# Half of the last matrix product by Strassen's seven block products, with its weight sums made in the opening

## The chip, the cores and the metric

The kernel runs on one core of a Trainium2 chip. Its engines are named as in the profile: PE (TensorE, matrix products), ACT (ScalarE), DVE (VectorE), POOL (GpSimd) and SP (SyncE, which here issues nearly all DMAs). Each runs its own list of instructions in order, and they meet through semaphores. The metric is the device time of one execution in microseconds (us), lower is better.

## The reference, cut to what matters

```python
h = _rmsnorm(x, g_pre)                       # x is 1024 x 1024, float32
proj = h @ w_in
...                                          # stick-breaking attention, gated linear attention
y_sb, y_gla = ... @ w_o_sb, ... @ w_o_gla
g_sb, g_gla = sigmoid(gate_logits + b_gate)  # two 1024 x 1024 gates
merged = g_sb * y_sb + g_gla * y_gla
x = x + merged @ w_out                       # the last product, 1024 x 1024 by 1024 x 1024
return _rmsnorm(x, g_final)
```

All is float32. The kernel gets there by splitting every operand into a high part (the PE's rounded fp32r form) and a low part (what is left of it), and by three passes: high by high, high by low, low by high. A product of a 128x128 block by a 128x512 block is so three matmuls.

## The kernel before, in words

The program has one hand-written instruction list for each engine. The stages are:

1. The opening (to about 59 us): x is loaded and normalised by rows (`row_norms` on ACT, `norm_rows` on DVE), turned by PE, and split into `h_hi` and `h_lo` (`h_high`, `h_low`). PE makes the first three column tiles of the projection (`first_tile`). POOL makes some constants.
2. The attention pairs, the gated linear attention, and the two products with `w_o`, whose outcome goes to a scratch in DRAM.
3. Seven of the eight tiles of the two gates (`gate_block(v, j)`, v from 0 to 6, j from 0 to 6). These already go by seven block products in place of eight. After each tile DVE merges: `mT` holds `merged` transposed, 8 blocks of 128 rows by 1024 columns, one block for each gate tile. Block 0 is the last to be finished. In the last gate tile SP also loads `w_out` in 8 chunks (`load_wout`), ACT makes the high parts (`wout_high`) and DVE the low parts (`wout_low`).
4. The last product: for each of 8 row tiles t and 2 column halves e, PE sums 8 blocks k in three passes, 24 matmuls of 128x512 into one bank of a ring of four (line 942). Before tile t, ACT splits columns 128 t to 128 t + 128 of `mT` into `m_hi` (line 1326) and DVE into `m_lo` (line 1837), two buffers in turn. The very first tile takes the blocks in the order 7 to 0, so that block 0 comes last; its piece of 128 columns is split apart (`split_m0(1)`, lines 1213 and 1741) as soon as DVE has merged block 0 (`merge_last`, lines 1844 and 1846). After each tile DVE adds x (`row_sum`, line 1861), ACT squares and sums the row and takes the root, DVE scales by it and by `g_final` (line 1875), SP stores.

What sets the order around the last product: PE waits for `mt_lo` (the low part of `mT`), for `wout_l` (the low part of `w_out`), and for `o5_free` (a bank read out). POOL has one instruction in this stage: it spreads `g_final` over the partitions (`partition_broadcast`, line 577), for which DVE waits (`fin_bc`).

POOL's operations do not all lie in the code that it holds at one time. The instruction order shows a row `ISA` with no operands where other code is called for: once ahead of the first `affine_select` (line 559) and once ahead of `partition_broadcast` (line 577). In the trace these are two records MODIFY_POOL_CONFIG each.

Of the kernel before, what the change touches and what calls it, by code (L numbers as in the profile page):

```python
# [12 lines left out]
P = 128  # L13
# [5 lines left out]
D = 1024  # L19
# [109 lines left out]
Y_LAST = 37  # L129
Y_SB_BANKS = 18  # L130
# [23 lines left out]
def stickbreak_gla_hybrid(nc, x, g_pre, w_in, b_gate, w_alpha_up, b_alpha_up, g_gla_norm,  # L154
# [8 lines left out]
    with ExitStack() as ctx:  # L163
# [98 lines left out]
        x_res = at("x_res", F + 20, [P, 2, D])  # L262
        y_row = at("y_row", F + 32, [P, 2, D])
        y_out = at("y_out", 8, [P, 2, D])
        g_fin = at("g_fin", F + 72, [P, D])
        junk5 = at("junk5", F + 76, [P, D])
        g_fin_row = at("g_fin_row", 4, [1, D])

        y_dram = nc.dram_tensor("y_scratch", (NP, 2, P, SEQ), F32, kind="Internal").ap()

# [101 lines left out]
        wout_l = sem("wout_l")  # L372
        fin_loaded = sem("fin_loaded")
# [38 lines left out]
        def _(sp):  # L412
# [19 lines left out]
            for c in range(8):  # L432
                sp.dma_start(w_up[RANK * c:RANK * (c + 1), :], w_alpha_up[0]).then_inc(up_loaded, 16)
# [75 lines left out]
            def load_wout(c):  # L509

                e, kk = c // 4, 2 * (c % 4)
# [16 lines left out]
            def store(t):  # L528
                for e in range(2):
                    es = slice(HALF * e, HALF * e + HALF)  # L530
                    sp.wait_ge(y_done, 2 * t + e + 1)
                    sp.dma_start(out_rows[t][:, es], y_out[:, t % 2, es]).then_inc(stored[t % 2], 16)
# [4 lines left out]
            for t in range(ST):  # L537
                if t >= 2:
                    sp.wait_ge(o5_free, 2 * (t - 2) + 2)
                else:  # L540
                    sp.wait_ge(prod_done, NP * NP)
                sp.dma_start(x_res[:, t % 2, :], x_rows[t]).then_inc(xr_loaded[t % 2], 16)
                if t >= 1:
                    store(t - 1)
            sp.wait_ge(tail_out, 1)
            sp.dma_start(out_rows[ST - 1][:, 0:HALF], y_out[:, 1, 0:HALF]).then_inc(stored[1], 16)
            sp.wait_ge(y_done, 2 * ST - 1)
            sp.dma_start(out_rows[ST - 1][:, HALF:D], y_out[:, 1, HALF:D]).then_inc(stored[1], 16)
            for s in stored:
                sp.wait_ge(s, 16 * ST)  # L550
# [807 lines left out]
        def _(dve):  # L1358
# [86 lines left out]
            for part in range(2):  # L1445
                stack(0, part, part)
# [468 lines left out]
```

## Time and profile before

| | us |
|---|---|
| median of 3 runs | 822.37 (822.10 to 822.48) |
| the profiled execution's own time | 822.67 |
| its span, first to last instruction | 820.9 |
| PE busy | 799.9, 97% of the span |
| DVE busy | 551.0, 67% |
| ACT busy | 394.8, 48% |
| POOL busy | 10.6, 1% |
| last product on PE, first matmul to last | 726.17 to 814.9 |

The profile is one execution. Busy times are sums; matmuls are pipelined, so a matmul that lasts 0.39 us in the records can follow the one before it after 0.23 us. What a stage costs on PE is therefore read from starts, not from durations. PE is busy nearly everywhere, so a cut of PE's work is a cut of the time as long as the other engines, the queue of DMAs and the semaphores deliver in time.

### The profile page before, as it was taken

How to read it: one execution, taken by the hardware profiler on the slowest of the kernel's cores; microseconds unless marked ns; L12 is line 12 of the kernel's file. 1: busy time of each engine (PE TensorE's matmuls, PEld its weight loads, DVE VectorE, ACT ScalarE, POOL GpSimd, SP SyncE). 2: the span in 40 equal slices, each digit the busy share in tenths (PEclk: the TensorE clock that was granted, in tenths of full speed). 3: DMA queues.
4: the chain of work that ended last, by engine and by line, in shares of the span. 5: the costliest groups of instructions: out<-in, count | busy, mean ns of one | idle time of the engine just before them, and what ended most of it. 6: DMA issues, size and time to landing. Idle time of an engine off the chain costs nothing.

```text
span 820.9 us, 11756 instructions
## 1 busy us (share of the span) xinstructions
PE 799.9 (97%) x4477; PEld 669.1 (82%) x4477; DVE 551.0 (67%) x776; ACT 394.8 (48%) x679; POOL 10.6 (1%) x16
## 2 busy tenths in 40 slices
PE   5999999999999999999999999999999999999997
PEld 4778888888888888879889888888888888878885
DVE  6528896989698698946545655665467776873332
ACT  8536675756666465654254153344333333542221
POOL 1000000000000000020000000000000000010000
PEclk9999999999999999999999999999999999999999
DMA  8122011212110220121110001243433444352321
GB/s 290 54 52 52 26 40 40 49 43 59 38 39 26 52 51 26 27 78 53 52 32 21 28 27 52 89 148 131 144 104 104 121 126 127 138 206 102 103 101 54
DMA packets 69714, 63.72 MB, mean 78 GB/s; under 512 B 3724, under 2 KB 57127, under 8 KB 69672
## 3 DMA queue, kind: packets, MB, share of 16 engines
q1 hardware_dynamic: 69618, 63.13, 25.1%
q8 instruction: 29, 0.48, 0.2%
q14 instruction: 13, 0.11, 0.0%
q10 hardware_dynamic: 54, 0.01, 0.0%
HBM read 47.40 MB, written 11.53 MB: 72 GB/s over the span
## 4 chain that ended last, share of the span: by engine, by line
PE 82%; DVE 10%; issue 3%; ACT 2%; DMA 2%; DVEq 0%; SPq 0%; ACTq 0%
PE pj L611 21%; PE ob L942 5%; PE ob L863 5%; PE sc L863 5%; PE sc L942 5%; PE tr L915 4%; PE pj L755 4%; PE ob L915 4%; DVE surv L1460 4%; PE pj L627 4%; PE pj L915 4%; PE ob L703 3%; PE sc L915 3%; PE tr L713 3%; PE pj L736 3%
## 5 line engine op out<-in xcount | busy, mean ns | idle before, releaser
L611 PE MATMUL pj<-h_hi,w_lo 128*128 128x512 f32 x336 | 134.2, 399 | 0.0
L611 PE MATMUL pj<-h_hi,w_hi 128*128 128x512 f32 x336 | 133.8, 398 | 0.0
L611 PE MATMUL pj<-h_lo,w_hi 128*128 128x512 f32 x336 | 133.7, 398 | 0.0
L1460 DVE TENSOR_TENSOR_SCAN surv<-surv 128x128 f32<-128x128 f32 (+3 forms) x64 | 86.5, 1351 | 19.2 <-ACT beta L1046 18.7
L611 PEld LDWEIGHTS pj<-h_hi,w_lo 128*128 128x128 f32 x336 | 63.5, 189 | 12.1 <-issue 0.5
L611 PEld LDWEIGHTS pj<-h_lo,w_hi 128*128 128x128 f32 x336 | 63.3, 188 | 12.1 <-issue 0.3
L611 PEld LDWEIGHTS pj<-h_hi,w_hi 128*128 128x128 f32 x336 | 63.5, 189 | 11.7 <-issue 0.2
L1087 ACT ACTIVATE wt_hi<-tr 128x512 fp32r<-128x512 f32 (+2 forms) x96 | 43.6, 490 | 43.2 <-PE tr L713 41.7
L1385 DVE TENSOR_TENSOR w_lo<-w_raw,w_hi 128x1024 fp32r<-128x1024 f32 x33 | 40.3, 1222 | 26.6 <-ACT w_hi L980 26.5
L1505 DVE TENSOR_TENSOR wt_lo<-tr,wt_hi 128x512 fp32r<-128x512 f32 (+2 forms) x96 | 50.1, 549 | 5.3 <-ACT wt_hi L1087 4.8
L1463 DVE TENSOR_TENSOR beta<-beta,surv 128x128 f32<-128x128 f32 (+3 forms) x64 | 48.6, 759 | 2.2
L1045 ACT ACTIVATE surv<-sc 128x128 f32<-128x128 f32 (+3 forms) x64 | 41.8, 654 | 13.8 <-PE sc L681 13.0
L713 PE MATMUL tr<-ident,beta 128*128 128x128 f32 x288 | 43.1, 277 | 4.0 <-DVE wt_lo L1505 4.0
L1046 ACT ACTIVATE beta<-sc 128x128 f32<-128x128 f32 (+3 forms) x64 | 41.6, 651 | 0.0
L713 PEld LDWEIGHTS tr<-ident,beta 128*128 128x128 f32 x288 | 32.4, 140 | 11.1 <-DVE wt_lo L1505 5.9
L980 ACT ACTIVATE w_hi<-w_raw 128x1024 fp32r<-128x1024 f32 x33 | 34.9, 1057 | 9.7 <-PE ob L863 9.3
L703 PE MATMUL ob<-wt_hi,v_st 128*128 128x256 f32 (+1 forms) x160 | 38.0, 272 | 0.5
L703 PE MATMUL ob<-wt_lo,v_st 128*128 128x256 f32 (+1 forms) x160 | 37.6, 282 | 0.0
L679 PE MATMUL sc<-k_hi,q_st 128*128 128x512 f32 (+2 forms) x96 | 37.1, 387 | 0.0
L755 PE MATMUL pj<-vn_hi,h_hi 128*128 128x256 f32 x128 | 36.5, 285 | 0.1
L755 PE MATMUL pj<-vn_hi,h_lo 128*128 128x256 f32 x128 | 36.4, 284 | 0.0
L755 PE MATMUL pj<-vn_lo,h_hi 128*128 128x256 f32 x128 | 36.3, 284 | 0.0
(326 smaller groups left out, 1868.2 us busy)
## 6 DMA issues: line engine op xcount, KB each, us to landing
w_raw<-in_w_in SPq DMA_DIRECT2D x30, 512.0 KB, 3.8
y_scratch<-y_ring SPq DMA_DIRECT2D x28, 256.0 KB, 2.0
graw<-in_w_in SPq DMA_DIRECT2D x14, 512.0 KB, 4.7
y_back<-y_scratch SPq DMA_DIRECT2D x14, 512.0 KB, 5.2
x_t<-in_x SPq DMA_DIRECT2D x8, 512.0 KB, 6.4
wout_raw<-in_w_out SPq DMA_DIRECT2D x8, 512.0 KB, 7.0
x_res<-in_x SPq DMA_DIRECT2D x8, 512.0 KB, 3.7
out_y<-y_out SPq DMA_DIRECT2D x16, 256.0 KB, 2.2
```

What stands on the lines that cost most here:

```text
L611: mm = pe.matmul(pj[bank][:, :], (w_lo if p == 2 else w_hi)[:, slot, k, :], (h_lo if p == 1 else h_hi)[:, k, HALF * h:HALF * h + HALF], st ...
L703: mm = pe.matmul(ob[gg % 2][:, c0:256], v_st[:, e, b, :], part[g % 2][:, b, c0:256], start=(b == 0 and part is wt_hi), stop=(b == blocks - ...
L713: mm = pe.transpose(tr[n % 2][:, P * b:P * b + P], beta[:, unit % 2, P * (b0 + b):P * (b0 + b) + P], ident[:, :])
L755: mm = pe.matmul(pj[c % 2][:, 256 * (t % 2):256 * (t % 2) + 256], (h_lo if p == 2 else h_hi)[:, k, P * t:P * t + P], (vn_lo if p == 1 else ...
L863: mm = pe.matmul(ring4[c % 4], (w_lo if p == 2 else w_hi)[:, slot, 4 * side + k, :], (g_lo if p == 1 else g_hi)[:, G_SLOT[4 * br + k], HAL ...
L915: mm = pe.matmul(bank_of, (gw_lo if p == 2 else gw_hi)[j][:, k, :], moving[j][p == 1][:, k, :], start=(j < 4 and k == 0 and p == 0), stop= ...
L942: mm = pe.matmul(ring4[c % 4], (m_lo if p == 2 else m_hi)[t % 2][:, k, :], (wout_lo if p == 1 else wout_hi)[e][:, u, :], start=(u == 0 and ...
L1045: act.activation(surv[:, step % 2, 0:keys], sc[:, 0:keys], ACT.Sigmoid, scale=-HD ** -0.5)
L1087: act.activation(wt_hi[g % 2][:, b0:b0 + nb, P * (unit % 2):P * (unit % 2) + P], tr[n % 2][:, 0:P * nb].rearrange("p (b q) -> p b q", q=P) ...
L1460: dve.tensor_tensor_scan(s[:, ::-1], s[:, ::-1], s[:, ::-1], 1.0, ALU.mult, ALU.bypass)\
L1463: dve.tensor_tensor(beta[:, step % 2, 0:keys], beta[:, step % 2, 0:keys], surv[:, step % 2, 1:keys + 1], ALU.mult).then_inc(w_ready, 1)
L1505: dve.tensor_tensor(wt_lo[g % 2][:, b0:b0 + nb, qs], tr[n % 2][:, 0:P * nb].rearrange("p (b q) -> p b q", q=P), wt_hi[g % 2][:, b0:b0 + nb ...
```

## The change

The last product is cut in two. Row tiles 0 to 3 are done as before, in another order: (t, e) is (0,1) (0,0) (1,1) (1,0) (2,1) (3,1) (2,0) (3,0). Row tiles 4 to 7 are done in two pairs (4 and 5, then 6 and 7). A pair's two row tiles and the two halves of the inner dimension are the four blocks of one operand, the four quarters of `w_out` those of the other, and seven products of 12 matmuls each (`out_block(p, o)`, o from 0 to 6) stand in place of eight.

- The four sums of quarters of `w_out` are made by POOL in the opening: SP loads `w_out` by rows in four parts of 1 MB (`load_wrow`), POOL makes 16 subtractions of 128x512, SP stores each group of four, 1 MB, to a scratch in DRAM (`store_wsum`). SP, ACT and DVE wait for all the stores ahead of the first attention pair. The 8 small loads of `w_up` go behind the first of these. In the last stage SP loads the sums back (`load_tw`, 4 of 1 MB) and ACT and DVE split them (`high_tw`, `low_tw`) beside row tiles 0 to 3.
- The sums of blocks of `mT` (two of them new, `os3` and `os2`, two in place) are made by POOL, 4 operations of 128x512 for each pair. The broadcast of `g_final` now stands between the second and the third of them.
- ACT's split of row tile 2 now waits for that broadcast and for `row_sum` 0 and 1, since the areas in use have moved.
- x is loaded into the place of the result, 4 rows of tiles instead of 2; its first load waits until the whole of `mT` is merged.
- The last gate tile is finished in pieces: 256 columns first (`last_part`, `finish_part`, `merge_a`, `merge_part`), then the split of block 0 for row tile 0, and the remaining 768 columns only after the remaining chunks of `w_out` and the split of row tile 1.
- In the opening the parts 4 to 7 of `h_high` and `h_low` go ahead of the split of the second weight tile instead of behind it.
- The end has other pieces: row tile 7 is normalised as a whole beside the last block product, row tile 6 in two halves.

POOL, before, from the constants of the middle of the program to its end (`mask_102` is a mask, `reset` and `sT` constants, `g_fin` the spread `g_final`):

```order
L565 MEMSET mask_102 128x512 [waits g_done]
L566 MEMSET reset 128x1024
L567 MEMSET sT 128x2048
L570 AFFINE_SELECT mask_102<-mask_102 128x512 [waits const_done]
L573 AFFINE_SELECT mask_102<-mask_102 64x512 [waits const_done]
L575 MEMSET reset 128x16
L577 ISA
L577 ISA g_fin<-g_fin_row 128x1024 [waits fin_loaded]
L163 UNCONDITIONAL_BRANCH
```

POOL, now, from the end of the same constants (`os_183` is `os3`, `os_184` is `os2`):

```order
L661 MEMSET reset 128x16
L670 TENSOR_TENSOR os_183<-mT 128x512 [waits m_step,m_ready]
L672 TENSOR_TENSOR mT<-mT 128x4x128 [waits os_ready]
L676 ISA
L676 ISA g_fin<-g_fin_row 128x1024 [waits fin_loaded,os_ready]
L678 ISA
L678 TENSOR_TENSOR os_184<-mT 128x512 [waits o5_ready]
L681 TENSOR_TENSOR mT<-mT,os_184 128x4x128 [waits om_low,os_ready]
L670 TENSOR_TENSOR os_183<-mT 128x512 [waits om_low]
L672 TENSOR_TENSOR mT<-mT 128x4x128 [waits os_ready]
L678 TENSOR_TENSOR os_184<-mT 128x512 [waits os_ready]
L681 TENSOR_TENSOR mT<-mT,os_184 128x4x128 [waits om_low,os_ready]
```

The broadcast has moved behind two additions that wait for the whole of `mT`, and a row `ISA` stands on each side of it.

ACT, before, where the last product begins, from the split of block 0 on (`m_hi0` and `m_hi1` are the buffers of even and odd row tiles, `wout_raw6` a loaded chunk of `w_out`):

```order
L1213 ACTIVATE m_hi0_153<-mT_112 128x128 [waits prod_done,m_step,m_ready]
L1205 ACTIVATE wout_hi1_150<-wout_raw6_147 128x1024 [waits prod_done,wout_loaded6]
L1205 ACTIVATE wout_hi1_150<-wout_raw7_148 128x1024 [waits prod_done,wout_loaded7]
L1326 ACTIVATE m_hi1_154<-mT_112 128x1024 [waits wout_l]
L1335 ACTIVATE junk5_161,stats_58<-y_row_158 128x1024 [waits o5_free]
L1338 ACT_TABLE_LOAD
L1338 ACTIVATE stats_58<-stats_58 128x1 [waits ss5]
L1326 ACTIVATE m_hi0_153<-mT_112 128x1024 [waits o5_ready]
```

ACT, now, at the same place:

```order
L1427 ACTIVATE gates2_139<-gates2_139,cols_56 128x256 [waits comb] x2
L1353 ACTIVATE m_hi0_153<-mT_112 128x128 [waits prod_done,m_step,m_ready]
L1345 ACTIVATE wout_hi1_150<-wout_raw6_147 128x1024 [waits prod_done,wout_loaded6]
L1345 ACTIVATE wout_hi1_150<-wout_raw7_148 128x1024 [waits prod_done,wout_loaded7]
L1476 ACTIVATE m_hi1_154<-mT_112 128x1024 [waits wout_l,prod_done]
L1476 ACTIVATE m_hi0_153<-mT_112 128x1024 [waits o5_ready,m_step,o5_free,fin_bc]
L1510 ACTIVATE junk5_188,stats_58<-x_res_186 128x1024
L1512 ACT_TABLE_LOAD
L1512 ACTIVATE stats_58<-stats_58 128x1 [waits ss5]
```

The split of row tile 2 (the second `m_hi0` of 128x1024 columns there) has gained the wait for `fin_bc`, which POOL gives with the broadcast.

The diff, cut to its core:

```diff
@@ SP, opening
-            for c in range(8):
-                sp.dma_start(w_up[RANK * c:RANK * (c + 1), :], w_alpha_up[0]).then_inc(up_loaded, 16)
+            load_wrow(0)
+            load_wrow(1)
             load(3, COL_Z, 1)
             load(4, COL_Q + P, 0)
+            for c in range(8):
+                sp.dma_start(w_up[RANK * c:RANK * (c + 1), :], w_alpha_up[0]).then_inc(up_loaded, 16)
+            store_wsum(0)
+            load_wrow(2)
+            store_wsum(1)
+            load_wrow(3)
+            store_wsum(2)
+            store_wsum(3)
             twin(0, 2)
             load(5, COL_K + P, 1)
+            for k in range(4):
+                sp.wait_ge(wsum_stored[k], 16)
@@ SP, last stage
+            sp.wait_ge(prod_done, NP * NP - 1)
+            load_tw(2)
+            sp.wait_ge(prod_done, NP * NP)
+            load_tw(3)
+            sp.wait_ge(m_step, 3 * NP + 5)
+            load_res(0)
+            sp.wait_ge(wout_l, KT)
+            load_tw(1)
+            if WHOLE_PAIRS == 2:
+                load_res(1)
...
@@ POOL
+            pool.wait_ge(x_normed, ST)
+            for k in range(4):
+                top, low = wrow[k % 2][:, 0, :], wrow[k % 2][:, 1, :]
+                ts = wsum[k]
+                pool.wait_ge(wrow_loaded[k % 2], 16 * (k // 2) + 16)
...
+                pool.tensor_tensor(ts[:, 0, :], top[:, HALF:D], top[:, 0:HALF], ALU.subtract).then_inc(wsum_done, 1)
+                pool.tensor_tensor(ts[:, 2, :], low[:, HALF:D], top[:, HALF:D], ALU.subtract).then_inc(wsum_done, 1)
...
-            pool.wait_ge(fin_loaded, 16)
-            pool.partition_broadcast(g_fin[:, :], g_fin_row[0:1, :], P).then_inc(fin_bc, 1)
+            pool.wait_ge(m_ready, 2)
+            pool.wait_ge(m_step, 3 * NP + 5)
+            for p in range(WHOLE_PAIRS, 4):
...
+                pool.tensor_tensor(os3[:, :, :], o11, o21, ALU.subtract).then_inc(os_ready, 1)
+                pool.wait_ge(os_ready, 4 * n + 1)
+                pool.tensor_tensor(o21, o21, o22, ALU.add).then_inc(os_ready, 1)
+                pool.wait_ge(os_ready, 4 * n + 2)
+                if n == 0:
+                    pool.wait_ge(fin_loaded, 16)
+                    pool.partition_broadcast(g_fin[:, :], g_fin_row[0:1, :], P).then_inc(fin_bc, 1)
+                    pool.wait_ge(o5_ready, 4 * WHOLE_PAIRS)
+                pool.tensor_tensor(os2[:, :, :], o21, o11, ALU.subtract).then_inc(os_ready, 1)
+                pool.wait_ge(os_ready, 4 * n + 3)
+                pool.wait_ge(om_low, NP * n + 1)
+                pool.tensor_tensor(o12, o12, os2[:, :, :], ALU.subtract).then_inc(os_ready, 1)
@@ PE
+            OUT_BANK = (0, 3, 1, 2, 1, 3, 2)
+            READ_BY = {4: 3, 5: 2, 6: 4}
+            def out_block(p, o):
...
+                if o in READ_BY:
+                    pe.wait_ge(pair_step, OP_STEPS * n + READ_BY[o])
...
+                for j in range(4):
+                    for q in range(3):
+                        mm = pe.matmul(bank_of, (om_lo if q == 2 else om_hi)[o][:, 3 - j, :],
+                                       out_moving[o][q == 1][:, j, :], ...)
@@ ACT, opening (DVE the same with h_low and low_part)
-            h_high(range(4))
+            h_high(range(KT))
             high_part(1, 1, 1, None, None)
-            h_high(range(4, KT))
@@ ACT, last stage
+            finish_part(0, 5 * NP)
+            finish_part(1, 5 * NP + 1)
             split_m0(1)
             wout_high(6)
             wout_high(7)
+            split_m(1)
+            act.wait_ge(fin_bc, 1)
+            act.wait_ge(o5_free, 2)
+            split_m(2)
+            square(0, 0)
+            act.wait_ge(o5_free, 4)
+            split_m(3)
...
@@ DVE, last stage
+            last_part(0)
+            merge_a(first)
+            last_part(1)
+            merge_part(first, 2 * NP, 3 * NP - 1)
             split_m0(1)
             for c in range(5, KT):
                 wout_low(c)
+            split_m(1)
+            merge_a(slice(256, SEQ))
+            merge_part(second, 2 * NP + 1, 3 * NP + 2)
+            merge_part(rest, 2 * NP + 1, 3 * NP + 4)
+            row_sum(0)
+            row_sum(1)
+            split_m(2)
...
```

## Rows read from the trace of the kernel before

**Rows 1.** The page: busy time and share of the span by engine.

```profile
PE   799.9 (97%) x4477; PEld 669.1 (82%) x4477; DVE 551.0 (67%) x776; ACT 394.8 (48%) x679; POOL 10.6 (1%) x16
```

**Rows 2.** Chain of waits, 700 to 821 us: start, duration, what (x count).

```profile
732.37 6.41 PE sc L942 x27
738.78 10.88 PE ob L942 x48
...
814.98 0.70 DVE y_row L1861
```

**Rows 3.** Timeline of PE, last product: start, duration, instruction, idle before and releaser.

```profile
726.17 0.39 PE L942 MATMUL sc<-wout_hi,m_hi 128*128 128x512 f32 x1
...
730.70 0.39 PE L942 MATMUL sc<-wout_hi,m_lo 128*128 128x512 f32 x1
732.37 0.50 PE L942 MATMUL sc<-wout_hi,m_hi 128*128 128x512 f32 x1 [1.28 <-DVE m_lo L1741]
```

**Rows 4.** Timeline of DVE, 732 to 736 us.

```profile
732.02 0.29 DVE L1741 TENSOR_TENSOR m_lo<-mT,m_hi 128x128 fp32r<-128x128 f32 x1 [0.42 <-ACT m_hi L1213]
732.23 3.49 DVE L1749 TENSOR_TENSOR wout_lo<-wout_raw,wout_hi 128x1024 fp32r<-128x1024 f32 x3
735.64 1.22 DVE L1837 TENSOR_TENSOR m_lo<-mT,m_hi 128x1024 fp32r<-128x1024 f32 x1
```

**Rows 5.** Timeline of ACT, 742 us: the split of one row tile.

```profile
742.21 1.04 ACT L1326 ACTIVATE m_hi<-mT 128x1024 fp32r<-128x1024 f32 x1
```

**Rows 6.** Timeline of POOL, whole program.

```profile
14.58 0.28 POOL L559 TENSOR_SCALAR_AFFINE_SELECT ident_bf<-ident_bf 128x128 bf16<-128x128 bf16 x1 [11.68 <-issue]
...
361.28 0.68 POOL L570 TENSOR_SCALAR_AFFINE_SELECT mask<-mask 128x512 f32<-128x512 f32 x1
362.02 1.58 POOL L573 TENSOR_SCALAR_AFFINE_SELECT mask<-mask 64x512 f32<-64x512 f32 x1
...
726.92 2.23 POOL L577 PARTITION_BROADCAST g_fin<-g_fin_row  x1 [363.25 <-DMA g_fin_row<-in_g_final]
```

**Rows 7.** Line 559: durations in ns, then first and last start.

```profile
L559 POOLq MODIFY_POOL_CONFIG  x2: 11/11/11, 3.1 to 3.1; - x2
```

**Rows 8.** The same for line 577.

```profile
L577 POOLq MODIFY_POOL_CONFIG  x2: 3/3/3, 363.8 to 363.9; - x2
```

**Rows 9.** Stretches of POOL: length, busy, granted clock, DMA share, GB/s.

```profile
9.00:14.50 5.50, 0.00 (x0) 1.00 1.10 362
...
740.00:750.00 10.00, 0.00 (x0) 1.00 0.32 105
```

**Rows 10.** Last stretch, all engines: the third number from the end is the granted clock.

```profile
819.00:820.90 1.90, 0.00 (x0) 0.00 (x0) 0.00 (x0) 0.00 (x0) 0.00 (x0) 0.67 0.53 203
```

**Rows 11.** Timeline of PE, opening.

```profile
7.09 0.69 PE L589 MATMUL tr<-ident,x_t 128*128 128x128 f32 x2
...
10.13 0.64 PE L589 MATMUL tr<-ident,x_t 128*128 128x128 f32 x2
10.56 0.45 PE L589 MATMUL ob<-ident,x_t 128*128 128x128 f32 x2
10.85 0.38 PE L589 MATMUL sc<-ident,x_t 128*128 128x128 f32 x2
```

**Rows 12.** Timeline of DVE and SP, the end.

```profile
817.05 0.75 DVE L1891 SCALAR_TENSOR_TENSOR y_out<-y_row,stats,g_fin 128x512 f32<-128x512 f32 x1
...
818.17 0.43 SPq L548 DMA_DIRECT2D out_y<-y_out  x1
```

**Rows 13.** Timeline of PE, ACT, DVE and SP, opening.

```profile
17.59 0.50 PE L627 MATMUL pj<-h_hi,w_hi 128*128 128x512 f32 x1 [0.21 <-DVE h_lo L1393]
...
17.58 1.11 ACT L962 ACTIVATE junk<-x_t 128x1024 f32<-128x1024 f32 x1
...
24.80 0.75 DVE L1380 TENSOR_SCALAR x_t<-x_t,stats 128x1024 f32<-128x1024 f32 x1
...
54.27 0.54 SPq L439 DMA_DIRECT2D k_hi<-k_hi  x1
```

More of the change, by code:

```diff
@@ L129 @@
 Y_LAST = 37
+OP_STEPS = 9
+WHOLE_PAIRS = 2
+WHOLE_TILES = ((0, 1), (0, 0), (1, 1), (1, 0), (2, 1), (3, 1), (2, 0), (3, 0))
 Y_SB_BANKS = 18
@@ L372, in stickbreak_gla_hybrid @@
         wout_l = sem("wout_l")
+        wrow_loaded = [sem("wrow_loaded0"), sem("wrow_loaded1")]
+        wsum_done = sem("wsum_done")
+        wsum_stored = [sem(f"wsum_stored{n}") for n in range(4)]
+        tw_high = sem("tw_high")
+        tw_low = sem("tw_low")
+        tw_loaded = [sem(f"tw_loaded{n}") for n in range(4)]
+        os_ready = sem("os_ready")
+        om_high = sem("om_high")
+        om_low = sem("om_low")
+        out_prod = sem("out_prod")
+        pair_step = sem("pair_step")
+        u2_copied = sem("u2_copied")
         fin_loaded = sem("fin_loaded")
@@ L535, in _, with store @@
+            def store(p, side, done):
+                sp.wait_ge(y_done, done)
+                sp.dma_start(out_rows[2 * p + side], x_res[:, 2 * (p % 2) + side, :]).then_inc(stored[p % 2], 16)
             sp.wait_ge(wout_l, 3)
             sp.dma_start(g_fin_row[0:1, :], g_final.rearrange("(a d) -> a d", a=1)).then_inc(fin_loaded, 16)
[L537 to L544, printed above, removed]
@@ L947, in _ @@
+            for p in range(WHOLE_PAIRS, 4):
+                for o in range(NP):
+                    out_block(p, o)
         @block.scalar
@@ L1035, in _ @@
             lr_quarters(1)
+            for k in range(4):
+                act.wait_ge(wsum_stored[k], 16)
             def pair(i, last):
@@ new lines, in _ @@
+            for p in range(WHOLE_PAIRS, 3):
+                row, done = 2 * (p % 2), OP_STEPS * (p - WHOLE_PAIRS)
+                for o in range(4):
+                    high_out(p + 1, o)
+                copy_u2(p)
+                for o in range(4, NP - 1):
+                    high_out(p + 1, o)
+                act.wait_ge(pair_step, done + 8)
+                square(2 * p, row + 1)
+                high_out(p + 1, NP - 1)
+                act.wait_ge(pair_step, done + 9)
+                square(2 * p + 1, row)
@@ L1449, in _ @@
             lr_quarters(1)
+            for k in range(4):
+                dve.wait_ge(wsum_stored[k], 16)
             dve.wait_ge(const_done, 1)
@@ L1850, in _ @@
+            first, second, rest = slice(0, 256), slice(256, HALF), slice(HALF, SEQ)
+            dve.wait_ge(comb, 5 * NP - 1)
+            last_part(0)
+            merge_a(first)
+            last_part(1)
+            merge_part(first, 2 * NP, 3 * NP - 1)
             split_m0(1)
@@ L1888, in _ @@
-            dve.wait_ge(ss5, done + 3)
+            split_m(1)
[5 more added lines that the diff above has]
+            split_m(2)
+            row_sum(2)
+            row_sum(3)
+            split_m(3)
+            dve.wait_ge(fin_bc, 1)
+            norm_row(0, 0)
+            norm_row(1, 1)
+            for o in range(2):
+                low_out(2, o, o)
```

392 lines of the change are left out of this document (287 added, 105 removed).

## The prediction, on record before the changed kernel ran

> **What bounds the kernel now.** I read the page first: PE is busy 97% of the span and no other engine over 67% [rows 1], so PE's list sets the time. The chain of waits over the last 120 us is PE's products, one after the other, from 732.37 to 814.98 us, and then a tail of reads, squares and stores [rows 2]. The timeline of PE around the first tile of the last product shows the one gap in it: 24 matmuls should follow evenly from 726.17, but the three of block 0 wait for its low part, from 730.70 to 732.37 [rows 3]. Then I read POOL's timeline, which nothing waits for today: 10.6 us of work in all. Two things in it matter for the change. Between its memsets at 2.9 us and the first affine_select there are 11.68 us in which it waits for nothing that the profile shows [rows 6], and two MODIFY_POOL_CONFIG records at 3.1 us stand at the start of that gap [rows 7]. The same pair stands ahead of the broadcast, at 363.8 us [rows 8]; there it costs nothing, since the broadcast waits for its row until 726.92 anyway. I read this pair as the fetching of other code for POOL. At every place where the instruction order shows an empty row ISA ahead of an operation I count one fetch.
>
> **What the change removes.** A matmul's step is 10.88 us over 48 = 0.2267 us [rows 2]. Before there are 8 row tiles x 48 = 384 matmuls. Now 4 x 48 = 192, and 2 pairs x 7 products x 12 = 168. 24 fewer x 0.2267 = 5.44 us, all on PE and so on the path.
>
> The gap in the first tile: 732.37 - 730.70 = 1.67 for a step of 0.23, so 1.44, and the 27 matmuls behind it take 6.41 where 27 x 0.2267 = 6.12, so 0.29 more. Together 1.73 us. In the new order block 0 is finished for 256 columns first. From the end of the last gate product, about 726.35, I have four DVE operations of 256 columns at about 0.42 (between 0.29 for 128 columns [rows 4] and 0.70 for 512 [rows 2]), with a sigmoid on ACT beside two of them; then one more 0.42, ACT's 128 columns at about 0.3, and DVE's 0.29 [rows 4]: some 729.3, where PE wants it at 730.93. The gap goes, with 1.6 us to spare. What is late next: chunks 5 to 7 of w_out take 3.49 us [rows 4] and end at 732.7, the last is wanted at about 735.7; the low part of row tile 1 ends at 734.0, wanted at 726.17 + 48 x 0.2267 = 737.05. Nothing of that is late. Gain 1.73.
>
> **What it adds on the path: the broadcast.** Row tile 2's split on ACT now waits for the broadcast. The list ahead of it: DVE merges the other columns, 768 at 0.95, twice 256 at 0.42, twice 512 at 0.7, from 734.0 to about 737.1. POOL then makes two additions of 128x512. The trace has no two-input operation on POOL; the nearest rows are 0.68 us for an affine_select of that shape and 1.58 for the odd one [rows 6], and I take 1.25, twice the first less an overhead: 739.6. Then comes the first of the two ISA rows. POOL runs its list in order, so the fetch can't begin before this point, unlike today. How long it is: 14.58 - 3.1 = 11.5 us in the opening, with the DMA engines at a share of 1.0 to 1.1 [rows 7, 9]. At 740 to 750 the share was 0.32 [rows 9], but the change puts 3 MB there (x of row tiles 0 to 3, and one 1 MB sum of w_out), 8.7 us at the opening's 362 GB/s. So most, not all, of this fetch is under the same load. Bounds: 0 if it is hidden, 11.7; I take 10, nearer the only row. 749.6. The broadcast 2.23 [rows 6]: 751.9. ACT's split 1.04 [rows 5] and DVE's 1.22 [rows 4], with 0.04 us for each of two semaphores: 754.2. PE wants row tile 2 at 726.17 + 4 x 5.44 = 747.9. It stands for 6.2 us (754.2 less 747.9, rounded down for the overlap of ends): from a fetch of F us the stall is F - 3.8. x for row tiles 0 and 1, loaded from 737.1 and there by about 742, is not what comes last.
>
> Behind the waiting split on ACT's list: the squares of row tiles 0 to 3, the split of row tile 3, the splits of the sums. They slide along with PE; row tile 3 is wanted 5.44 us after tile 2, and ACT and DVE need 1.04 + 1.2 + 1.6 + 1.04 + 1.22, some 6 us less what ACT did first, so it is just in time. The second ISA row (back to the code for additions) fetches from 751.9 to about 762; its addition is wanted only when PE has done 8 tiles, at 775.9. Hidden.
>
> **The clock after such a stall.** After PE's last matmul, at about 814.9, the granted clock stays 1.00 and falls only in the last stretch, where its mean is 0.67 over 1.9 us [rows 10]: one level, 2.4 to 1.2 GHz, at about 819.65, so 4.7 us after PE's last work. After the 1.67 us gap of today nothing fell. In the opening PE starts at 7.09 with 0.215 us for each transpose, and goes to 0.11 only at about 10.6 [rows 11]: 3.5 us at half speed, 1.8 us lost. A stall of 6.2 us is longer than 4.7, so I count the fall and 1.8 us for the way back.
>
> **What is hidden.** (1) POOL's 16 subtractions in the opening start when x is normalised, 24.80 + 0.75 [rows 13], and take 16 x 1.25 = 20 us, some 7 more for the two loads of 1 MB that wait for a buffer, and 5 for the last store: about 53. SP's copy of k at 54.27 [rows 13] and the first pair at 59 wait for them. It holds up to about 1.8 us for an addition; above that each 0.1 us costs 1.6 on the path. The code is that of affine_select, as no ISA row stands between. (2) The order of h_high and the second weight: PE's wait at 17.59 [rows 13] goes, 0.4 us, but ACT's row sums begin 0.6 us later than 17.58, and the last normalised tile, ready at 25.5 today, is what PE waits for at 26: I count 0, between -0.4 and +0.3. (3) In the block products PE needs from DVE the reading of bank 1 (READ_BY 4: 3). DVE reads it 2.7 us ahead; by my count of its list (splits at 0.62, sums at 0.62 apart, one row normalised at 1.4) it is done 1.5 to 2 us in time.
>
> **The tail.** Today the last product's end is followed by 814.98 to 817.80 (0.75 from 817.05) and a store issued at 818.17 [rows 12]. Now row tile 7 (three DVE operations that end 0.65 before PE's end) occupies ACT for 1.2 + 0.3 and DVE for 1.6 more; the last half of row tile 6 comes 0.6 us later than in today's order, and its store goes behind 512 KB more: 0.7 us.
>
> **Sum.** -5.44 - 1.73 + 6.2 + 1.8 + 0.7 = +1.5 us. The profiled execution took 822.67 (span 820.9 and 1.77 around it), 0.3 above the median of 822.37. On the median: 823.9 us.
>
> By the Trainium skill (GPSIMD Engine Reference, section 2.1 "Instruction dispatch") the first call to freshly loaded code pays about 6 us for the load of instruction memory. The trace's only row has 11.5 with the DMAs full. By the page's figure the stall would be 2.2 and the clock would stay, so the sum would be -5.44 - 1.73 + 2.2 + 0.7 = -4.3: 818.1 us. It is an estimate from the page and is rival B below, whose price I work out from rows.
>
> **Rivals.**
> A, the forecast, a fetch of 8.7 to 11.7 us with the fall of the clock: stall 4.9 to 7.9, 822.5 to 825.6, up to 826.3 if the half speed lasts longer. Chance 0.50.
> A2, the same stall, but the clock holds: 1.8 less, 822.1 at the middle, 820.7 to 823.8. One fall after 4.7 us is all the rows show. Chance 0.13.
> B, the fetch is much shorter than in the opening, since its length there came from full DMA engines, which I can't tell from one row: half of 11.5 gives a stall of 2.0, 817.9; 8 us gives 4.2, 820.1. Chance 0.21.
> C, there is no exposed fetch: the change does not do what I read into the ISA rows, or it runs ahead of the additions. -5.44 - 1.73 + 0.7 = -6.5: 815.9. For it: rows 8 show no length. Chance 0.06.
> D, slower by POOL's additions themselves. If one takes 2.0 us and not 1.25, the opening's stores end at about 62 and the first pair waits 3 us, and the two additions ahead of the broadcast add 1.5: 823.9 + 4.5 = 828.4. It decides from 1.8 us on. For it: rows 6 have an operation at 1.58. A part of it would also come where DVE and POOL read the SBUF at once, between the last whole tile and the first block products: DVE's 1.5 to 2 us to spare there are used up by two additions that hold it. Chance 0.10.
>
> On that last point the Trainium skill (SBUF — State Buffer, section "SBUF: two separate sides") says that a DVE operation with two SBUF inputs and a GpSimd operation exclude each other for a whole instruction. No row here shows the two at once, since POOL is idle then.
>
> **Numbers.** This kernel can be told from no change from about 0.2%, 1.64 us: 820.7 and 824.0. Faster: B, C and a little of A2, 0.28. Within: 0.11 of A2 and 0.18 of A, 0.29. Slower: the rest of A and D, 0.43. The likeliest case's own range is 822.3 to 826.3. Over the cases the range goes from 818.3 (within B) to 827.0.
>
> **What would show it.** Right: two MODIFY_POOL_CONFIG records at about 739.6 with POOL idle for 8 to 12 us before the broadcast; ACT's split of row tile 2 waiting for POOL; one PE wait of 5 to 8 us at 748; a granted clock of 0.5 in the 3 or 4 us behind it; no PE wait at 731; 168 matmuls in the block products at 0.227 each and no wait within them; POOL's stores in the opening landed before 59. Wrong: a broadcast at 742, which is C; matmuls at full speed right behind the stall, A2; the pair's first scores later than 59, D; or a wait of PE for pair_step or om_low, which I have at nothing.

## The result, and the profile after

The changed kernel takes 825.1 us (median of 19 runs, 823.21 to 826.90), the kernel before 822.57 beside it on the same chip (19 runs). The ratio is 1.0028, 95% interval 1.0022 to 1.0035: slower by 2.3 us (1.8 to 2.9). The profiled execution took 826.43 us (span 824.7). A second profile of the same kernel, taken later (e12_changed_again), took 825.22.

The page of the changed kernel: busy time by engine. PE's 24 matmuls are gone, but its busy time is that of [rows 1], 799.6 for 799.9.

```profile
PE 799.6 (97%) x4453; PEld 668.1 (81%) x4453; DVE 572.0 (69%) x801; ACT 407.8 (49%) x700; POOL 43.1 (5%) x40
```

PE's waits (us in total, times, the longest) show one that the kernel before did not have, the low part of row tile 2 (line 2062):

```profile
PE sc L1045 <- DVE m_lo L2062: 5.2, 1, 5.2
```

The timeline of POOL around it (start, duration, what, idle before and its end), and POOL's records for the broadcast's line:

```profile
739.48 1.29 POOL L670 TENSOR_TENSOR os<-mT 128x512 f32<-128x512 f32 x1 [373.13 <-DVE mT L2082]
740.85 1.29 POOL L672 TENSOR_TENSOR mT<-mT 128x512 f32<-128x512 f32 x1
752.09 1.30 POOL L676 PARTITION_BROADCAST g_fin<-g_fin_row  x1 [9.95 <-issue]
```

```profile
L676 POOLq MODIFY_POOL_CONFIG  x2: 11/11/11, 742.1 to 742.1; - x2
```

The two additions end at 742.14, the pair MODIFY_POOL_CONFIG stands there, and nothing runs on POOL for 9.95 us. The chain of waits goes through that gap:

```profile
740.85 1.30 POOL mT L672
742.14 9.94 issue
752.09 1.31 POOL g_fin L676
753.40 0.02 issue
753.42 1.06 ACT m_hi L1476
754.49 0.02 issue
754.51 1.24 DVE m_lo L2062
755.75 0.14 issue
755.88 12.90 PE sc L1045 x48
768.79 10.88 PE ob L1045 x48
```

Row tile 2 was wanted at 728.81 (first matmul of the last product here) + 96 x 0.2267 = 750.57 and begins at 755.88, a stall of 5.31 us. The 48 matmuls behind it take 12.90 where the next 48 take 10.88 (as in [rows 2]), 2.02 us more. Of this 0.27 is not the clock: where PE waits and the clock holds, the 48 behind the wait take 11.15 and 11.16 (e2_pe_filled and e3_quiet_dma below). So 1.75 us go to the clock. Stretches of the changed kernel (from:to, length, busy time of PE, PEld, DVE, ACT, POOL, granted clock, DMA share, GB/s):

```profile
740.00:748.00 8.00, 8.00 (x37) 6.64 (x36) 1.29 (x2) 0.00 (x0) 2.06 (x2) 1.00 0.96 367
748.00:751.00 3.00, 2.73 (x13) 1.91 (x11) 0.00 (x0) 0.00 (x0) 0.00 (x0) 1.00 0.18 72
751.00:755.90 4.90, 0.02 (x1) 0.05 (x1) 1.39 (x2) 2.46 (x4) 1.30 (x1) 0.68 0.00 0
755.90:758.00 2.10, 2.10 (x5) 1.72 (x6) 1.03 (x2) 2.09 (x4) 0.00 (x0) 0.50 0.00 0
758.00:760.00 2.00, 2.00 (x7) 1.53 (x7) 1.86 (x3) 1.97 (x6) 0.00 (x0) 0.60 0.00 0
760.00:762.00 2.00, 2.00 (x10) 1.65 (x9) 1.97 (x3) 2.00 (x4) 0.00 (x0) 1.00 0.21 86
```

The granted clock falls to half (1.2 of 2.4 GHz) while PE stands, about 2 us after PE's last work, and comes back some 3.7 us after it goes on. The DMA engines were full for the first 6 of the fetch's 9.95 us (share 0.96 from 740 to 748, where 740 to 750 had 0.32 before [rows 9]), and nearly idle for its last 4. The wait at 731 of [rows 3] is gone, and the block products go at 12 in 2.72 us with no wait.

In the second profile the same places read: stall 5.35 (wanted 748.59, begun 753.94), fetch 10.11, the 48 behind it 13.64, so 2.76 more, 2.49 of it for the clock. The clock is at half from 752.4 to 759.2 us there and from 752.8 to 759.6 in the first profile. Since PE went on at 753.94 and at 755.88, its matmuls ran at half speed for 5.3 us in the second and for 3.7 in the first.

```profile
750.15 1.30 POOL L676 PARTITION_BROADCAST g_fin<-g_fin_row  x1 [10.11 <-issue]
```

```profile
753.81 0.14 issue
753.94 13.64 PE sc L1045 x48
767.59 10.88 PE ob L1045 x48
```

### The profile page after: what moved, and what is told of

Its sections match the earlier page's. It is cut to its first block, busy times and chain, and to the rows that moved or that the text cites. A ratio compares the mean times of both kernels' runs of the same rounds, so it can differ in the third digit from the quotient of the medians.

```text
span 824.7 us, 11834 instructions
## 1 busy us (share of the span) xinstructions
PE 799.6 (97%) x4453; PEld 668.1 (81%) x4453; DVE 572.0 (69%) x801; ACT 407.8 (49%) x700; POOL 43.1 (5%) x40
## 4 chain that ended last, share of the span: by engine, by line
PE 78%; DVE 10%; issue 5%; ACT 3%; DMA 2%; POOL 0%; SPq 0%; DVEq 0%; ACTq 0%; POOLq 0%
PE pj L715 21%; PE ob L967 5%; PE sc L967 5%; PE tr L1019 4%; PE pj L859 4%; PE ob L1019 4%; DVE surv L1684 4%; PE pj L1019 4%; PE pj L731 3%; PE ob L807 3%; PE sc L1019 3%; PE tr L817 3%; PE pj L840 3%; PE sc L784 2%; PE sc L783 2%
```

## The experiments

Each is timed against the kernel before on its own chip. Where two kernels were timed on different chips, I compare their ratios. The "kernel with the broadcast first" is e1_bc_early.

### e1_bc_early: the broadcast ahead of the additions

```diff
+            pool.wait_ge(fin_loaded, 16)
+            pool.partition_broadcast(g_fin[:, :], g_fin_row[0:1, :], P).then_inc(fin_bc, 1)
             pool.wait_ge(m_ready, 2)
             pool.wait_ge(m_step, 3 * NP + 5)
...
-                    pool.wait_ge(fin_loaded, 16)
-                    pool.partition_broadcast(g_fin[:, :], g_fin_row[0:1, :], P).then_inc(fin_bc, 1)
```

> The changed kernel with the broadcast of g_final ahead of POOL's additions on mT, so that its code is fetched while POOL idles in the middle of the program. Theory 1 (the 5.2 us wait of PE at row tile 2 and the 3.3 us of matmuls at half clock behind it come from the code fetch): both go, 5.2 + 1.7 = 6.9 us less than the changed kernel's 825.1, so 818.2, no PE wait after 726 us; the second fetch lies between 729 and 739 and hides nothing. Rival 2 (ACT's split waits as long for x and row_sum, or for the second fetch): at most 2 us less, 823 or more. Rival 3 (the block products' gain was eaten elsewhere, by the opening): the wait goes and the time is still within 1 us of the kernel before.

Measured: 816.41 us (816.09 to 817.11), ratio 0.9926 (0.9914 to 0.9939), 6.1 us under the kernel before and, by the two ratios, 8.4 under the changed one; I had expected 6.9. The stall and the matmuls behind it are 7.3 and 8.1 of it in the two profiles; the rest is of the size by which the opening differs (see e12_changed_again). Its timeline of POOL, and the records of the broadcast's line:

```profile
726.40 1.44 POOL L663 PARTITION_BROADCAST g_fin<-g_fin_row  x1 [363.22 <-DMA g_fin_row<-in_g_final]
736.84 1.29 POOL L672 TENSOR_TENSOR os<-mT 128x512 f32<-128x512 f32 x1 [9.01 <-DVE mT L2082]
```

```profile
L663 POOLq MODIFY_POOL_CONFIG  x2: 3/3/3, 363.1 to 363.1; - x2
```

The switch of code stands at 363 again, ahead of a long wait, and the switch back falls into the 9.01 us before `mT` is whole. PE has no wait from 726 on. This is the version that beats both kernels: the place of two lines is worth about 8.4 us. A second timing of it on another chip (e10_bc_early_again) gave 817.30, ratio 0.9928 (0.9915 to 0.9941).

### e2_pe_filled: PE kept at work ahead of the stall

```diff
+                if c == 4:
+                    for _ in range(20):
+                        pe.matmul(pj[0][:, :], wout_hi[0][:, 0, 0:P], wout_hi[0][:, 1, :], ...)
```

> The changed kernel with 20 extra matmuls of 128x512 on PE between the fourth and the fifth tile of the last product, into a bank that is overwritten later: 4.5 us of work inside the 5.2 us wait. Theory 1 (the idle PE lets the granted clock fall, and this costs 1.7 us on the way back): the clock stays at 1.00 up to the end, 825.1 - 1.7 = 823.4. Rival (the slow matmuls behind the wait are a refill of the pipeline, whatever the clock): 825.1, within 0.3.

Measured: 823.36 us, ratio 1.0007 (0.9998 to 1.0015). The granted clock is 1.00 from 726 to 780 us. PE's waits are now

```profile
PE sc L1049 <- DVE m_lo L2066: 1.6, 1, 1.6
PE pj L1081 <- DVE x_res L2178: 0.7, 1, 0.7
```

20 x 0.2267 = 4.5 us of idle matmuls and these two waits are 6.8 of the 6.95 us over e1_bc_early. The 48 matmuls behind the wait take 11.15 us, where the two profiles of the changed kernel have 12.90 and 13.64. So the slow matmuls were the clock's, and the rival is out. What this is worth in the whole time is less clear. By the ratios the kernel is 1.7 us faster than the changed one. But from the first matmul of the last product to PE's end it takes 89.2 us, beside 88.9 and 89.7 in the two profiles of the changed kernel, since its fetch took 11.07 us and since PE meets a second wait, of 0.7 us for a bank in the block products.

### e3_quiet_dma: the large loads held back while the code is fetched

```diff
             sp.wait_ge(wout_l, KT)
+            sp.wait_ge(fin_bc, 1)
             load_tw(1)
```

> The changed kernel, but SP issues the load of one weight sum (1 MB) and x of row tiles 2 and 3 (1 MB) only after the broadcast, so that most of the fetch runs with idle DMA engines. Theory B (the fetch is long because the DMA engines are full): the fetch falls from 10.0 to about 6 us, PE's wait from 5.2 to 1 to 2 us with the clock up, 825.1 - 5.5 = 819.6. Theory A (its length is its own): 9 to 10 us again, 825.1 within 0.5.

Measured: 817.82 us, ratio 0.9943 (0.9932 to 0.9955). Stretches and POOL's timeline:

```profile
738.00:741.00 3.00, 3.00 (x15) 2.49 (x14) 0.00 (x0) 0.00 (x0) 1.29 (x1) 1.00 0.81 309
741.00:744.00 3.00, 3.00 (x15) 2.49 (x14) 1.29 (x2) 0.00 (x0) 0.00 (x0) 1.00 0.01 3
```

```profile
744.98 1.30 POOL L677 PARTITION_BROADCAST g_fin<-g_fin_row  x1 [5.63 <-issue]
```

With the DMA engines quiet from 741 on, the fetch takes 5.63 us and not 9.95, PE waits 0.7 and the clock holds. Only the loads differ, so the 4.3 us more in the changed kernel come from them: the fetch takes longer beside full DMA engines. Theory A said 825.1, and it fell; theory B said 819.6, and by the ratios the gain is 7.0 us where it had 5.5.

### e4_before_late: the exposed fetch alone, in the kernel before

```diff
+            pool.wait_ge(m_step, 3 * NP + 2)
+            pool.memset(late[:, :], 0.0).then_inc(const_done, 1)
             pool.wait_ge(fin_loaded, 16)
             pool.partition_broadcast(...)
```

> The kernel before, with one small memset on POOL that waits until mT is merged (731.6 us) put ahead of the broadcast, so that its code is fetched only then; nothing else is changed. Theory 1: broadcast done at 731.7 + 10 + 1.3 = 743.0, low part of row tile 1 at 744.3 in place of 736.9, PE wants it at 738.8: a wait of 5.6 us and 1.7 us for the clock, 822.6 + 7.3 = 829.9. Rival (the place of the fetch costs nothing by itself): 822.6.

Measured: 824.25 us, ratio 1.0019 (1.0010 to 1.0028), where I had 829.9. POOL:

```profile
731.99 0.10 POOL L578 MEMSET late<- 128x1 f32 x1 [368.64 <-DVE mT L1849]
737.96 1.30 POOL L580 PARTITION_BROADCAST g_fin<-g_fin_row  x1 [5.87 <-issue]
```

The DMA share is 0.01 from 732 to 735 and 0.00 to 738, and the fetch takes 5.87 us. I had used 10 us again. With 5.87 the wait is 4.1 us shorter and the clock holds, which is about the 5.7 us that I was off, and it is the second case of a short fetch with idle DMA engines. PE waits 1.4 us more.

### e5_opening_only: the opening's part alone, in the kernel before

```diff
+            load_wrow(0)
+            load_wrow(1)
...
+            for k in range(4):                        # POOL, 4 subtractions each
+                pool.wait_ge(wrow_loaded[k % 2], 16 * (k // 2) + 16)
...
+            for k in range(4):                        # SP, ACT and DVE
+                sp.wait_ge(wsum_stored[k], 16)
```

> The kernel before, with the opening's part of the change alone: w_out loaded by rows in four parts of 1 MB, POOL's 16 subtractions, four stores of 1 MB, the 8 small loads of w_up moved behind the first loads, and the waits of SP, ACT and DVE for the stores. The sums are not used; the last product and the order of h_high are as before. Theory 1 (the prediction's): all of it lies beside PE's work, the last store lands before SP, ACT or DVE come to their waits, at about 53 us; 822.5 us, within 0.3 of before. Rival: loads and stores hold up other loads of the opening or the three waits bite; 1 us or more, 823.5 and above, with PE's first scores of the first pair later than 58.9. On POOL's code: since this kernel still ends with the broadcast's code on POOL, I expect the first affine_select at about 14.6 us again, as in the kernel before, and not at 3.4 as in the changed kernel, which ends with the additions' code.

Measured: 823.47 us for 823.55, ratio 1.0001 (0.9992 to 1.0010). The loads, subtractions and stores cost nothing that can be told. The first affine_select comes at 15.25 here, and in the changed kernel at 3.39:

```profile
15.25 0.28 POOL L588 TENSOR_SCALAR_AFFINE_SELECT ident_bf<-ident_bf 128x128 bf16<-128x128 bf16 x1 [12.35 <-issue]
```

```profile
3.39 0.29 POOL L631 TENSOR_SCALAR_AFFINE_SELECT ident_bf<-ident_bf 128x128 bf16<-128x128 bf16 x1 [0.49 <-POOL mask_neg L629]
```

### e6_h_order_back: the old order of h_high and h_low

```diff
-            h_high(range(KT))
+            h_high(range(4))
             high_part(1, 1, 1, None, None)
+            h_high(range(4, KT))
```

> The kernel with the broadcast first (e1_bc_early), with the opening's order of h_high and h_low as before the change: parts 0 to 3, the second weight tile, parts 4 to 7. Theory 1 (the prediction's term): the order is worth nothing, 0 between -0.4 and +0.3; 816.4. Rival (from the two traces: SP's copy of k stands at 53.86 us where it stood at 54.27, and PE's wait of 0.2 for h_lo at 17.59 is gone): the new order gains 0.4 us, so this kernel takes 816.8.

Measured: 816.79 us, ratio 0.9919 (0.9906 to 0.9933). Inconclusive: against e1_bc_early's 0.9926 (0.9914 to 0.9939), on another chip, neither a gain nor a loss of 0.4 us can be told. The 0.4 us that I read as a gain from two profiles is no more than what the opening varies.

### e7_one_piece and e11_as_before_block0: how block 0 is finished

e7 merges 512 columns at once ahead of the split, and e11 also multiplies all 1024 columns first. Neither goes all the way back: the kernel before merges both halves, all 1024 columns, ahead of the split (`merge_last(1, 1)` and `merge_last(0, 3)`), and e11 only the first. So what is said of e11 below, that block 0 is finished as in the kernel before, does not hold for its edit.

```diff
-            merge_a(first)
             last_part(1)
-            merge_part(first, 2 * NP, 3 * NP - 1)
+            merge_a(slice(0, HALF))                       # e11: slice(0, SEQ)
+            merge_part(slice(0, HALF), 2 * NP + 1, 3 * NP - 1)
```

> The kernel with the broadcast first (e1_bc_early), with 512 columns of block 0 merged at once ahead of the split for row tile 0, instead of 256 first (the other 512 follow later, as the 768 did). Theory 1 (the prediction's term of 1.73 us): block 0's low part comes about as late as in the kernel before, PE waits 1.3 us at 731 again; 816.4 + 1.7 = 818.1. Rival: the gap had gone for another reason, such as the split's place ahead of the other columns; then PE does not wait and it stays at 816.4.

> The kernel with the broadcast first, with block 0 finished as in the kernel before: one product over all 1024 columns first, then 512 columns merged, then the split for row tile 0. In e7_one_piece, with that product over 512 columns, PE waited 0.4 us at 731.3 and stepped 0.1 slower once. Theory 1: the 1.73 us of the prediction were the sum of both parts of the reordering; the longer product (1.23 for 0.69 us) brings the wait to 1.0 or more, and the kernel takes 1.2 to 1.7 us more than e10_bc_early_again. Rival: something else in the list of the last gate tile took the gap away, and this kernel is no slower than e7_one_piece (0.6 over e1_bc_early).

Measured: e7 817.43 us, ratio 0.9921 (0.9908 to 0.9934), e11 817.70, ratio 0.9931 (0.9919 to 0.9943), beside 817.30 for e10_bc_early_again, which ran on e11's chip. Differences of 0.5 us can't be told by these times; the timeline of PE answers the question. In e7 and in e11 the matmul behind the low part of block 0 starts at

```profile
731.73 0.50 PE L1045 MATMUL sc<-wout_hi,m_hi 128*128 128x512 f32 x1 [0.25 <-DVE m_lo L1965]
```

```profile
732.19 0.50 PE L1045 MATMUL sc<-wout_hi,m_hi 128*128 128x512 f32 x1 [0.53 <-DVE m_lo L1965]
```

where it would be due at 731.32 and 731.50: 0.41 and 0.69 us, and 0.11 more for the first step, 0.5 and 0.8 in all. I expected 1.3 in e7 and 1.0 or more in e11. The timelines of DVE show why it was less. Ahead of the split, the kernel before has the first half's two operations and then the second half's:

```profile
728.49 1.06 DVE L1844 TENSOR_TENSOR gates<-gates,y_back 128x512 f32<-128x512 f32 x1
729.58 0.69 DVE L1846 TENSOR_TENSOR mT<-mT,gates 128x512 f32<-128x512 f32 x1
730.19 0.69 DVE L1844 TENSOR_TENSOR gates<-gates,y_back 128x512 f32<-128x512 f32 x1
730.91 0.69 DVE L1846 TENSOR_TENSOR mT<-mT,gates 128x512 f32<-128x512 f32 x1
```

e11 has the first half's alone:

```profile
729.04 1.65 DVE L2080 TENSOR_TENSOR gates<-gates,y_back 128x512 f32<-128x512 f32 x1
730.73 0.69 DVE L2082 TENSOR_TENSOR mT<-mT,gates 128x512 f32<-128x512 f32 x1
```

The second half puts the split off by 0.61 + 0.72 = 1.33 us, counted from start to start. That is an estimate of what it has in the gap of 1.44 us in [rows 3], so nearly all of it. And the waits in e7 and e11 are not those of the pieces alone: one operation that takes 0.69 us by itself takes 1.65 in e11, and 1.54 in e7, while POOL's broadcast runs from 728.41 and from 729.17. The changed kernel has no broadcast there. What 256 columns are worth against 512, without the broadcast beside, no run shows.

### e8_more_sums and e9_two_more_sums: how much POOL work the opening holds

```diff
+                for n in (1, 3):                      # e8 in all four groups, e9 in the last one
+                    pool.tensor_tensor(ts[:, n, :], low[:, HALF:D], top[:, HALF:D], ALU.subtract).then_inc(more, 1)
...
```

> The kernel with the broadcast first (e1_bc_early), with 8 more subtractions of 128x512 in the opening, two in each group of four, written to places that are written again: 8 x 1.29 = 10.3 us more on POOL, as if each of the 16 took 1.93 us. The last store then lands at 53 + 10.3 = 63.3 us. Theory 1 (the prediction's rival D, its rule: free up to 1.8 us for one, above that 16 times the excess): 16 x 0.13 = 2.1 us, 818.5. Theory 2 (by the trace: ACT's first work of the pair stands at 60.2 and waits for the last store, and the copy of k and the next weight load stand behind it on SP): 63.3 - 60.2 = 3.1 us for ACT at least, up to 9.4 for the load of the weights, which stood at 55.1 and goes at 64.4: 3 to 5 us, 819.4 to 821.4. Theory 3, the opening has more room than that: below 1 us.

> The kernel with the broadcast first (e1_bc_early), with 2 more subtractions of 128x512 in the last group of the opening only: 2.6 us more on POOL, as if each of the 16 took 1.45 us. Theory 1 (the prediction's rule, free up to 1.8 us for one): nothing, the same as e10_bc_early_again. Theory 2 (from e8_more_sums, where PE waited 8.1 us for the copy of k after SP had issued that copy 7.0 us later): the room is the 0.9 us between the last store's landing, at about 53, and SP's copy at 53.9, and the copy itself has none; PE waits 1.7 to 2.0 us for k_lo and the kernel takes 1.7 to 2.2 us more than e10_bc_early_again.

Measured: e8 827.37 us, ratio 1.0053 (1.0037 to 1.0069), by the ratios about 10 us over e1_bc_early, more than any theory had. e9 817.48, ratio 0.9928 (0.9915 to 0.9940), the same as e10_bc_early_again. PE's wait in e8, its last operations on POOL, and SP's copy of k:

```profile
PE sc L787 <- DMA k_lo<-k_lo: 8.1, 1, 8.1
```

```profile
52.28 4.59 POOL L647 TENSOR_TENSOR wsum<-wrow 128x512 f32<-128x512 f32 x2
56.94 2.16 POOL L650 TENSOR_TENSOR wsum<-wrow,wsum 128x512 f32<-128x512 f32 x1
59.18 1.26 POOL L652 TENSOR_TENSOR wsum<-wrow,wsum 128x512 f32<-128x512 f32 x1
```

```profile
60.88 0.54 SPq L478 DMA_DIRECT2D k_hi<-k_hi  x1
```

The copy stands on SP behind the issue of the last store, which waits for the last subtraction; it does not wait for that store's landing, as both the prediction and my theory for e9 had it. In e1_bc_early the last subtraction ends at 48.8 and the copy goes at 53.9, so 5 us are free, 0.31 for each of 16: by this count the limit is 1.6 us for one, not 1.8. In e9 the last one ends at 52.3, still in time. In e8 it ends at 60.4, also because its last subtractions run beside DVE (two of them take 4.59 us, earlier two 2.53); the copy goes at 60.9, lands 5.8 us after its issue (3.8 in e9) because it shares the DMA engines with the last store, and PE stands 8.1 us. The clock falls as well, to half while PE stands:

```profile
65.00:67.40 2.40, 0.01 (x1) 0.02 (x1) 0.00 (x0) 1.49 (x2) 0.00 (x0) 0.50 0.95 228
```

### e10_bc_early_again, e12_changed_again

> The kernel e1_bc_early again, word for word, as the base of the two others on this chip: 6.1 us under the kernel before, ratio 0.9926.

> The changed kernel again, word for word, for a second profile. In its first profile the last product began 2.6 us later than before, all of it lost in the opening, and the fetch of code took 9.95 us; with both, the terms add up to that execution's 826.4 us. The median was 825.1. Theory 1: the late opening is chance from one execution to the next (e10_bc_early_again had 2.1 us of it, e1_bc_early none), and the fetch is about 11 us, as in e2_pe_filled: this profile then shows the last product at 726 to 727, a wait of 6 us or more at row tile 2, and 825 us. Theory 2: the late opening belongs to this kernel: the last product at 728 or later again, the wait 5.2 us.

Measured: e12 825.60 us, ratio 1.0031 (1.0019 to 1.0043). Its last product begins at 726.83, and at 728.81 in the first profile, so the late opening is not fixed to this kernel, as theory 2 had it; its other half, a wait of 5.2 us, came true. The fetch was not 11 us, so that half of theory 1 is out.

Where the late start comes from can be read in PE's opening. Of the first profile's 2.64 us all stand there already at the first projection matmul behind a group of transposes. The changed kernel's first profile, and for the last line e1_bc_early's, which starts the last product at 725.64:

```profile
17.71 0.63 PE L731 MATMUL pj<-h_lo,w_hi 128*128 128x512 f32 x1
18.13 0.63 PE L731 MATMUL pj<-h_hi,w_lo 128*128 128x512 f32 x1
19.09 0.47 PE L731 MATMUL pj<-h_hi,w_hi 128*128 128x512 f32 x1
```

```profile
15.93 0.48 PE L731 MATMUL pj<-h_hi,w_hi 128*128 128x512 f32 x1
```

That matmul is at 19.09 there, at 17.12 in e12, 16.44 in the kernel before and 15.93 in e1_bc_early, and from it to the last product it is 709.7 us in all four. From 15.15 to 18.56 us PE steps at 0.43 us a matmul in the first profile, the step of half speed, and at 0.23 in e1_bc_early from 13.74 on. (The record of the granted clock reads 1.00 in both; the steps do not.) In the two profiles with the latest starts, this one and e10_bc_early_again, PE stood for 0.7 us at about 10.8 before its steps had become short, waiting for a normalised tile. So what these profiles lose in the opening is PE's later rise to full speed; why it waited there longer, no run shows. In the profiles with the opening's new order of h_high the last product starts between 725.64 and 728.81 (nine profiles, e8 left out); in the four with the old order (before, e4, e5, e6) between 726.17 and 726.31. Whether the new order makes the opening less steady stays open.

## Why the prediction was right, and where it was not

The mechanism was right: one stall at row tile 2 behind a code fetch of about 10 us, with a fall of the clock, eats what the block products gain. The size of the total, forecast at 1.5 us over the kernel before and measured at 2.3, is in part luck, since the stall was put 0.9 us too long and the opening at nothing. From the 822.67 us of the profile before, both profiles come out if the later start of the last product, which the prediction had at 0, is put in as measured. First: 2.64 later at the start of the last product - 5.44 - 1.73 + 5.31 + 2.02 + 0.95 (tail) = 826.42, measured 826.43. Second: 0.66 - 5.44 - 1.73 + 5.35 + 2.76 + 0.95 = 825.22, measured 825.22. Without the first number in each, the terms give 1.1 and 1.9 us over the kernel before.

- **Matmuls, -5.44.** Right: the block products step at 2.72 us for 12.
- **Gap at 731, -1.73.** Right in size and place: no wait in the changed kernel. The low part of block 0 ended 1.8 us before PE wanted it, where the prediction had 1.6. Most of the gap was the second half of the columns, 1.33 us by the timeline of DVE, which all these kernels leave until after the split.
- **Stall, +6.2.** 5.3. The fetch was 9.95 and 10.11 us for my 10. The broadcast took 1.30 us, not the 2.23 of [rows 6], which is nearly the whole difference; the other links of the chain were off by 0.3 us or less each. It takes 1.30 in all five profiles in which DVE is idle beside it (the changed kernel's two, e2, e3, e4), and up to 2.23 beside DVE's operations of two operands, as in the last gate tile of the kernel before. The addition took 1.29 us (I had 1.25, between 0.68 and 1.58).
- **Clock, +1.8.** 1.75 and 2.49, with 0.27 more behind any such wait, which the prediction had left out. Right to count it: A2 is out. The rows had one fall 4.7 us after PE's last work; here it came after 2.1 and 3.7 us. The price depends on how much of the half speed falls into the stall, so that one number for it was too simple.
- **Tail, +0.7.** PE's end to the end of the span is 5.95 us before and 6.9 in e1_bc_early (807.40 to 814.3): 0.95. It is 6.9 in both profiles of the changed kernel too.
- **Opening, 0.** As for the work put there, right: e5_opening_only, which has all of it but the new order of h_high, is within 0.1% of the kernel before. The changed kernel's two profiles still start the last product 2.64 and 0.66 us late (see e12). The prediction's time of 53 us for the last store does not follow from its parts: 25.55 + 20 + 7 + 5 is 57.6. In e1_bc_early the additions end at 48.8, because POOL waits 2.5 us for a load and not 7, so the 53 was near by luck. The point from which POOL's additions cost was 1.6 and not 1.8 us, and its price beyond is steeper than 16 times the excess (10 us in e8 for additions that ended 11.6 later), since the copy's landing gets slower and the clock falls.
- **Rival B** was right about the mechanism and wrong about this kernel. The fetch is longer beside full DMA engines: 5.63 and 5.87 us when they are quiet for most or all of it, 9.95 to 12.35 when they are full for its first 6 us or longer (share 0.99 to 1.06). But the change itself fills them, as the prediction's count of 3 MB said, so the long fetch came. The Trainium skill (GPSIMD Engine Reference, section 2.1 "Instruction dispatch") has about 6 us for the first call to freshly loaded code; the traces with quiet DMA engines agree (5.6 and 5.9), and those with full ones take nearly twice as long.
- **Rival C** is what e1_bc_early makes of the change: 815.9 forecast for no exposed fetch, 816.4 measured.
- **Rival D.** DVE and POOL do hinder each other: an addition is 1.29 us alone and 1.6 to 2.2 beside DVE in the block products, but in the changed kernel no wait of PE came of it. (In e2, where the block products come closer behind row tile 2, PE waits 0.7 us for a bank there, which the prediction had at nothing; its chain leads back to a weight sum that landed at 771.4 us, not to POOL's additions.) The Trainium skill (SBUF — State Buffer, section "SBUF: two separate sides") has a DVE operation with two SBUF inputs and a GpSimd operation that reads SBUF exclude each other for a whole instruction; the trace shows longer additions, which fits, and no cost on the path here. The changed kernel:

```profile
779.76 2.21 POOL L678 TENSOR_TENSOR os<-mT 128x512 f32<-128x512 f32 x1 [26.37 <-PE ob L1045]
782.06 1.29 POOL L681 TENSOR_TENSOR mT<-mT,os 128x512 f32<-128x512 f32 x1
784.58 1.68 POOL L670 TENSOR_TENSOR os<-mT 128x512 f32<-128x512 f32 x1 [1.23 <-DVE om_lo L2102]
```

So 7.2 us were gained as meant, and 7.3 to 8.1 given back by one instruction's place in POOL's list, with 1 us of tail and a later start on top.

## What to carry to other kernels

When an engine gets a new kind of operation, look in its list for where its code is switched, and put each switch ahead of a wait that is long anyway; the instruction that a fast engine waits for must not stand behind one. A long stall of PE can cost the clock on top, here 1.7 to 2.5 us behind one of 5.3, so a stall is not priced by its length alone. When you undo part of a change to price it, check in the timeline that the old order is really back, and what else now runs beside it: e11 was meant to be the old order and was not. Before filling idle transfer time, see what small thing is fetched or copied beside it: here a code fetch and a copy of k both took 1.5 to 2 times as long.

## What the runs showed of the hardware

- POOL's code stays from one execution to the next. Kernels that end with the additions' code start their first affine_select at 3.39 us (eleven profiles), kernels that end with the broadcast's at 14.58 [rows 6], 14.21 (e4) and 15.25 (e5, which has the additions in its opening too). The kept code gained nothing here, since nobody waits for it. The pair MODIFY_POOL_CONFIG stands at 3.1 to 3.3 us in all of these profiles, so the pair alone does not show a fetch.
- affine_select and the two-input addition share one code, the broadcast is in another, and a memset needs no switch (e4: 731.99 behind nothing, then the fetch).
- A fetch of POOL's code: 5.87 us at a DMA share of 0.00 (e4) and 5.63 at 0.20, all of it in the first 2 us (e3). In the last stage 9.95, 10.11 (e12) and 11.07 us (e2), with a share of 0.99 to 1.01 in the first 6 us and of 0.26 or less after. In the opening 11.32 (e4), 11.68 [rows 6] and 12.35 (e5) at 1.03 to 1.06. Within the busy cases the length does not follow the share.
- An addition of two 128x512 float32 operands on POOL: 1.29 us, up to 2.35 beside DVE. The broadcast: 1.30 us, up to 2.23 beside DVE. It goes both ways: DVE's operation of 0.69 us took 1.65 beside the broadcast (e11).
- The granted clock fell to half in stalls of 5.3 us (twice) and of 8.1 us, and in none of the shorter ones (1.6 us and less).
